# Two adaLN pairs of the second layer computed during the routing of the first layer's experts

## The reference, cut to what matters

```python
def trunk(x, cond, P, caches):
    for l in range(2):
        mod = silu(cond) @ P['ada_w'][l] + P['ada_b'][l]          # (1024) @ (1024, 6144)
        sh1, sc1, g1, sh2, sc2, g2 = split(mod, 6)
        h = x * (1.0 + sc1) + sh1
        out = even_mixer(h, ...) if l % 2 == 0 else hyena_mixer(h, ...)   # hyena: u = h @ hy_w_in ...
        x = layer_norm(ALPHA * x + g1 * out, ln_w[l, 0], ln_b[l, 0])
        h = x * (1.0 + sc2) + sh2
        y = moe_ffn(h, router_w, router_bias, moe_w_gate[l], moe_w_up[l], moe_w_down[l])
        x = layer_norm(ALPHA * x + g2 * y, ln_w[l, 1], ln_b[l, 1])
```

## Time and profile before

| | us |
|---|---|
| median of 3 runs | 1306.19 |
| lowest, highest | 1302.87, 1306.76 |
| the profiled execution | 1303.92 |
| its span, first to last instruction | 1302.2 |
| TensorE busy | 991.1 (76%) |
| VectorE busy | 415.4 (32%) |
| ScalarE busy | 228.1 (18%) |
| GpSimd busy | 164.3 (13%) |
| read from memory | 320.50 MB |

### The profile page before, as it was taken

The page is one execution under the profiler, slowest core; times in us unless marked ns, Lnnn a source line. Parts: engine busy times, 40 slices in busy tenths (PEclk is TensorE's granted clock), DMA queues, the critical chain, the costliest instruction groups (busy, mean ns, idle before and its releaser), DMA issues.

```text
span 1302.2 us, 23736 instructions
## 1 busy us (share of the span) xinstructions
PE 991.1 (76%) x9370; PEld 553.3 (42%) x9370; DVE 415.4 (32%) x1135; ACT 228.1 (18%) x455; POOL 164.3 (13%) x323
## 2 busy tenths in 40 slices
PE   1899998698289759794489999898938997775830
PEld 0444446554245435352245554445424553332510
DVE  0220117855422212121453234553541221111207
ACT  0401002513212111121221111110321211110202
POOL 1200001100221111112020000001022111110121
PEclk9999999799689989898799998899958998887965
DMA  9995324577379999999994113633631969999973
GB/s 323 374 306 204 105 108 137 195 310 290 152 281 388 395 396 394 404 367 390 392 377 150 45 60 104 257 130 138 254 158 41 329 245 393 401 407 404 391 275 133
DMA packets 78858, 345.06 MB, mean 265 GB/s; under 512 B 8086, under 2 KB 8537, under 8 KB 66508
## 3 DMA queue, kind: packets, MB, share of 16 engines
q1 hardware_dynamic: 57108, 289.30, 57.6%
q0 software_dynamic: 13648, 43.84, 9.9%
q10 hardware_dynamic: 8040, 11.01, 2.5%
HBM read 320.50 MB, written 23.63 MB: 264 GB/s over the span
## 4 chain that ended last, share of the span: by engine, by line
PE 57%; DMA 23%; DVE 11%; ACT 3%; issue 2%; SPq 2%; POOL 1%; POOLq 0%; ACTq 0%; DVEq 0%; PEldq 0%
DMA ring<-in_moe_w_up_dram 15%; PE bank L830 15%; PE bank L636 11%; PE bank L895 10%; PE bank L759 6%; PE bank L837 6%; DMA ring<-in_ada_w_dram 5%; PE bank L589 2%; SPq L1323 2%; DMA ring<-in_moe_w_down_dram 1%; PE bank L969 1%; PE bank L993 1%; ACT arena L1181 1%; PE bank L907 1%; DVE arena L1292 1%
## 5 line engine op out<-in xcount | busy, mean ns | idle before, releaser
L830 PE MATMUL bank<-ring,arena 128*32 128x256 f32 x3072 | 193.9, 409 | 51.7 <-DMA ring<-in_moe_w_up_dram 49.5
L830 PEld LDWEIGHTS bank<-ring,arena 128*32 128x32 f32 x3072 | 105.0, 118 | 133.4 <-issue 76.1
L636 PE MATMUL bank<-ring,hT 128*128 128x512 f32 x336 | 144.9, 593 | 1.0 <-ACT hT L1029 1.0
L1290 DVE TENSOR_TENSOR arena<-arena,bank 128x64 f32<-128x64 f32 x136 | 27.4, 201 | 316.1 <-ACT arena L1181 316.1
L895 PE MATMUL bank<-hT,ring 128*128 128x384 f32 x384 | 124.6, 487 | 1.0 <-ACT hT L1029 1.0
L837 PE MATMUL bank<-ring,arena 128*32 128x256 f32 x1536 | 92.8, 382 | 27.5 <-DVE arena L1292 25.4
L589 PE MATMUL bank<-ring,small 128*32 128x256 f32 x768 | 55.5, 453 | 62.1 <-DMA ring<-in_ada_w_dram 62.1
L636 PEld LDWEIGHTS bank<-ring,hT 128*128 128x128 f32 x336 | 63.6, 190 | 80.6 <-issue 79.3
L895 PEld LDWEIGHTS bank<-hT,ring 128*128 128x128 f32 x384 | 72.7, 190 | 52.5 <-ACT hT L1029 1.2
L830 PE MATMUL bank<-arena 128*32 128x256 f32 x1216 | 74.3, 399 | 14.8 <-DMA arena<-in_moe_w_up_dram 14.8
L837 PEld LDWEIGHTS bank<-ring,arena 128*32 128x32 f32 x1536 | 45.1, 109 | 58.6 <-DVE arena L1292 31.9
(11 more groups left out here) (316 smaller groups left out, 1093.9 us busy)
## 6 DMA issues: line engine op xcount, KB each, us to landing
ring<-in_ada_w_dram SPq DMA_DIRECT2D x24, 2048.0 KB, 19.1
ring<-in_moe_w_gate_dram SPq DMA_DIRECT2D x22, 2048.0 KB, 22.0
ring<-in_moe_w_up_dram SPq DMA_DIRECT2D x22, 2048.0 KB, 27.0
ring<-in_moe_w_down_dram SPq DMA_DIRECT2D x22, 2048.0 KB, 29.9
arena<-in_moe_w_gate_dram SPq DMA_DIRECT2D x10, 2048.0 KB, 35.6
arena<-in_moe_w_up_dram SPq DMA_DIRECT2D x10, 2048.0 KB, 41.3
arena<-in_moe_w_down_dram SPq DMA_DIRECT2D x10, 2048.0 KB, 44.3
ring<-in_ev_w_in_dram SPq DMA_DIRECT2D x7, 2048.0 KB, 16.4
```

The costliest lines, as they stand in the source:

```text
L636: last = pe.matmul(bank[3 * (c % 2) + t], hT[:, k, t * P:(t + 1) * P], slot8(n)[:, k, :], start=k == 0, stop=k == KT - 1)
L830: last = pe.matmul(bank[1][q * BLK:(q + 1) * BLK, 0:HALF], slot_inT[:, k, :], both[:, :, k, q * P:(q + 1) * P], start=k == 0, stop=k == KT ...
L1290: dve.tensor_tensor(act_rows[:, two, :], silu_g[:, two, :], up, ALU.mult).then_inc(S["gated"], 1)
```

## The change

The four chunks of pairs (1,0) and (1,1) move from the head of `BETWEEN` to the end of `BEFORE`. They are loaded to slots 4, 6, 7 and 8: the three last ones where expert 2 was loaded before, the first to slot 4 once the mixer's output is through with it. Both pairs are computed within `pe_moe` of layer 0, behind the position counts and the token copies, in banks 3, 4 and 2. Their rows can't lie in slot 5, which an expert takes, so they are written to the head of `hT`, whose content the token copies have used up. Expert 0, expert 1's gate and expert 1's down are loaded as before the routing; expert 1's up and expert 2's three matrices wait for the ada matmuls. In `BETWEEN` the slots of the later chunks shift, so that the chunks of (1,2) and (1,3) now have slots 3, 4, 0, 1 and come first. In the gap only (1,2) and (1,3) are left; the copies of (1,0) and (1,1) are gone from `act_ln`, (1,2) is copied before the wait for tile 0's scale, and the columns of (1,3) are made behind the modulate.

```diff
--- before.py
+++ after.py
@@ -65,8 +65,9 @@
 
 
 BEFORE = (pair_chunks(0, 0) + pair_chunks(0, 1) + matrix_chunks("ev_in", 0, 3) + pair_chunks(0, 3) + matrix_chunks("ev_in", 3, 7)
-          + pair_chunks(0, 2) + pair_chunks(0, 4) + pair_chunks(0, 5) + matrix_chunks("ev_out", 0, 2))
-BETWEEN = (pair_chunks(1, 0) + pair_chunks(1, 1) + pair_chunks(1, 2) + pair_chunks(1, 3) + matrix_chunks("hy_in", 0, 6)
+          + pair_chunks(0, 2) + pair_chunks(0, 4) + pair_chunks(0, 5) + matrix_chunks("ev_out", 0, 2)
+          + pair_chunks(1, 0) + pair_chunks(1, 1))
+BETWEEN = (pair_chunks(1, 2) + pair_chunks(1, 3) + matrix_chunks("hy_in", 0, 6)
            + pair_chunks(1, 4) + pair_chunks(1, 5) + matrix_chunks("hy_out", 0, 2))
 MOE0 = len(BEFORE)
 HYBRID1 = MOE0 + 3 * NE
@@ -76,8 +77,8 @@
 
 def ring_slots():
 
-    slots = [(i + 4) % STAGING for i in range(len(BEFORE))] + [i % MOE_RING for i in range(3 * NE)]
-    slots += [(i + 3) % STAGING for i in range(len(BETWEEN) - 5)] + [0, 1, 2, 3, 4] + [i % MOE_RING for i in range(3 * NE)]
+    slots = [(i + 4) % STAGING for i in range(len(BEFORE) - 4)] + [4, 6, 7, 8] + [i % MOE_RING for i in range(3 * NE)]
+    slots += [(i + 3) % STAGING for i in range(len(BETWEEN) - 6)] + [3, 4, 0, 1, 3, 4] + [i % MOE_RING for i in range(3 * NE)]
     seen = [0] * MOE_RING
     held, full, before = [None] * MOE_RING, [], []
     for n, slot in enumerate(slots):
@@ -569,10 +570,13 @@
         def dve_proj_count(c):
             return sum(2 if k in ROPED else 0 for k in range(c + 1))
 
+        def mod_row_of(l, q):
+            return at(q * HALF, HALF, src=hf) if l == 1 and q < 2 else mod_rows[q]
+
         def act_ada(act, l, q, b):
 
             act.wait_ge(ada_mm, ADA_ORDER.index((l, q)) + 1)
-            act.activation(mod_rows[q], b[:, 0:HALF], ACT.Copy).then_inc(mod_row, 1)
+            act.activation(mod_row_of(l, q), b[:, 0:HALF], ACT.Copy).then_inc(mod_row, 1)
 
         def pe_condition(pe):
             pe.wait_ge(cond_act, 1)
@@ -598,7 +602,7 @@
 
             pe.wait_ge(mod_row, ADA_ORDER.index((l, q)) + 1)
             for j in range(2):
-                last = pe.transpose(b[:, j * P:(j + 1) * P], mod_rows[q][:, j * P:(j + 1) * P], ident)
+                last = pe.transpose(b[:, j * P:(j + 1) * P], mod_row_of(l, q)[:, j * P:(j + 1) * P], ident)
             last.then_inc(modT_mm, 1)
 
         def dve_ada_columns(dve, l, q, b):
@@ -813,6 +817,11 @@
                 last = pe.matmul(bank[6][:, NT * NE:(NT + 1) * NE], ones, mask[:, s, :], start=s == 0, stop=s == NT - 1)
             last.then_inc(pos_mm, 1)
             pe.wait_ge(htok_act, 6 * (l + 1))
+            if l == 0:
+                pe_ada(pe, 1, 0, bank[3])
+                pe_ada(pe, 1, 1, bank[4])
+                pe_ada_columns(pe, 1, 0, bank[2])
+                pe_ada_columns(pe, 1, 1, bank[3])
             pe.wait_ge(table_rdy, l + 1)
             pe.wait_ge(trips_rdy, l + 1)
 
@@ -887,6 +896,7 @@
                     pe.wait_ge(hy_dve, c - 2)
                 if c == 2:
                     pe.wait_ge(dft_in, 16 * 4)
+                    pe.wait_ge(modT_rdy, COLUMN_PAIRS.index((1, 3)) + 1)
                     pe.matmul(bank[7][0:FH, 0:T], w1, feat, start=True, stop=True).then_inc(fmm, 1)
                 if c == 5:
                     pe.wait_ge(fsin, 1)
@@ -1040,21 +1050,17 @@
 
         def act_ln(act, n):
             j = n // 2
-            if n == 1:
-                act_ada(act, 1, 0, bank[0])
             for t in range(NT):
-                if n == 1 and t == 2:
-                    act_ada(act, 1, 1, bank[1])
                 act.wait_ge(gathered[t], 32 * (j + 1))
                 act.activation(ln_sum(n, t), ln_sum(n, t), ACT.Copy, scale=wsel[:, 0, t:t + 1]).then_inc(ln_first, 1)
             for t in range(NT):
                 act.wait_ge(ln_var, NT * j + t + 1)
                 act.activation(sd[:, t:t + 1], mv[:, t, 1:2], ACT.Sqrt, bias=eps_col, scale=1.0).then_inc(ln_sd, 1)
                 if t == 0:
+                    if n == 1:
+                        act_ada(act, 1, 2, bank[2])
                     act.wait_ge(ln_rstd, j + 1)
                     act.activation(ln_sum(n, 0), ln_sum(n, 0), ACT.Identity, bias=nmr[:, 0:1], scale=rstd[:, 0:1]).then_inc(ln_nrm, 1)
-                    if n == 1:
-                        act_ada(act, 1, 2, bank[2])
             if n == 1:
                 act_ada(act, 1, 3, bank[7])
 
@@ -1170,6 +1176,9 @@
                 act.wait_ge(htok_mm, 6 * l + u + 1)
                 act.activation(h_tok[:, u // 2, :].rearrange("p (k j s) -> p j s k", k=KT, j=KT)[:, u % 2 * 4:u % 2 * 4 + 4],
                                bank[u].rearrange("p (j s k) -> p j s k", j=4, k=KT), ACT.Copy).then_inc(htok_act, 1)
+            if l == 0:
+                act_ada(act, 1, 0, bank[3])
+                act_ada(act, 1, 1, bank[4])
             act.wait_ge(trips_rdy, l + 1)
             act.sem_inc(S["stored0"], 32)
             act.sem_inc(S["stored1"], 32)
@@ -1278,6 +1287,9 @@
             link(dve.tensor_reduce(places[:, FIRST:NE], square, AX, ALU.add))
             link(dve.tensor_scalar(places[:, FIRST:NE], places[:, FIRST:NE], -1.0, float(NE), ALU.mult, ALU.add))
             dve.tensor_copy(order[0:1, FIRST:NE], places[0:1, FIRST:NE]).then_inc(order_rdy, 1)
+            if l == 0:
+                dve_ada_columns(dve, 1, 0, bank[2])
+                dve_ada_columns(dve, 1, 1, bank[3])
             dve.wait_ge(trips_rdy, l + 1)
             pairs = dve.value_load(trips[0:1, 1:2], min_val=NE // 2, max_val=MAX_BLOCKS // 2)
 
@@ -1330,21 +1342,42 @@
                 else:
                     sp.wait_ge(MS[layer]["down_mm"], ends)
 
+            def staging_free(layer):
+                sp.wait_ge(modT_mm, 4 * (layer + 1))
+                sp.wait_ge(gate_out[2 * layer], 64)
+                sp.wait_ge(gate_out[2 * layer + 1], 64)
+
+            def first_experts():
+
+                gap = chunk_at("ada", 1, 0)
+                for j in range(3):
+                    sp.wait_ge(*used(PREVIOUS[MOE0 + j]))
+                    expert_matrix(sp, 0, 0, MOE0, j)
+                sp.wait_ge(cT_mm, KT)
+                sp.wait_ge(out_done, 16 * OUT_DMAS)
+                for n in range(gap + 1, gap + 4):
+                    sp.dma_start(slot8(n), chunk_src(n)).then_inc(ring_full[SLOT[n]], 16)
+                sp.wait_ge(*used(PREVIOUS[MOE0 + 3]))
+                expert_matrix(sp, 0, 1, MOE0 + 3, 0)
+                load(gap)
+                staging_free(0)
+                expert_matrix(sp, 0, 1, MOE0 + 3, 2)
+                for e, j in ((1, 1), (2, 0), (2, 1), (2, 2)):
+                    sp.wait_ge(*used(PREVIOUS[MOE0 + 3 * e + j]))
+                    expert_matrix(sp, 0, e, MOE0 + 3 * e, j)
+
             def load_moe(layer, first):
 
-                for e in (0, 2, 1):
-                    if e == 2 and layer == 0:
-                        sp.wait_ge(cT_mm, KT)
-                        sp.wait_ge(out_done, 16 * OUT_DMAS)
-                    if e == 2 and layer == 1:
+                if layer == 0:
+                    first_experts()
+                for e in (0, 2, 1) if layer else ():
+                    if e == 2:
                         sp.wait_ge(inv_dve, KT)
                         sp.wait_ge(lnrow_in, ROWS_DUE[2])
                     for j in range(3):
                         n = first + 3 * e + j
                         if SLOT[n] == STAGING:
-                            sp.wait_ge(modT_mm, 4 * (layer + 1))
-                            sp.wait_ge(gate_out[2 * layer], 64)
-                            sp.wait_ge(gate_out[2 * layer + 1], 64)
+                            staging_free(layer)
                         elif SLOT[n] < STAGING:
                             sp.wait_ge(*used(PREVIOUS[n]))
                         expert_matrix(sp, layer, e, first + 3 * e, j)
@@ -1363,7 +1396,7 @@
                         next_expert(three * 3 + group, group)
                 next_expert(NE - 1, 0)
 
-            for n in range(MOE0):
+            for n in range(MOE0 - 4):
                 load(n)
             load_moe(0, MOE0)
             for n in range(HYBRID1, MOE1):
@@ -1444,14 +1477,10 @@
             pe_projections(pe)
             pe_mixer(pe)
             pe_moe(pe, 0, MOE0)
-            pe_ada(pe, 1, 0, bank[0])
-            pe_ada(pe, 1, 1, bank[1])
-            pe_ada_columns(pe, 1, 0, bank[0])
             pe_ada(pe, 1, 2, bank[2])
-            pe_ada_columns(pe, 1, 1, bank[1])
             pe_ada(pe, 1, 3, bank[7])
+            pe_modulate(pe, 2)
             pe_ada_columns(pe, 1, 3, bank[7])
-            pe_modulate(pe, 2)
             pe_hyena(pe)
             pe_moe(pe, 1, MOE1)
 
@@ -1733,9 +1762,8 @@
             dve_tiles(dve, link, 0)
             dve_moe(dve, link, 0)
             dve_ln(dve, link, 1)
-            for q, b in ((0, 0), (1, 1), (3, 7)):
-                dve_ada_columns(dve, 1, q, bank[b])
             dve_modulate(dve, 2)
```

(1 more changed line is left out.)

## The result

The changed kernel takes 1311.26 us (median of 20 runs), the kernel before 1306.32 us (20 runs): ratio 1.0043, 95% interval 1.0027 to 1.0059, so 3.5 to 7.7 us slower. The forecast was 1310.5, +4.5. The profiled execution of after was timed at 1313.39 us, its span is 1311.7. In its trace everything stands 1.8 us later already where the first scatter is issued (345.08 instead of 343.32). Executions differ by as much there without any change: in experiment 7, whose edit lies wholly behind this place, the scatter is issued at 345.92. So I compare places by their distance from that issue.

A forecast was written before the change was run, and what follows sets the result against it. Bound by waits for ada weights between the first expert layer and the projection, a 65.9 us gap. Scatters' delay +19.5 minus gap gain 15.0 is +4.5 on 1306.2: 1310.7, rounded to 1310.5 us, range 1298.5 to 1316.5.

The forecast's parts named there:

- The loads beside the scatters: In the routing, four late expert matrices take turns by packet with the scatters, which end 19.5 us later.
- The share by bytes: Rival, 20 in 100: scatters get half the bytes in the routing, start +11.0 us, net -4.0, 1302.2 us.
- the scatters' right of way: Rival, 11 in 100: scatters hardly slowed in the routing, expert layer on time, four matrices late; middle -11.5, 1294.7 us.
- the fetch's 4.6 us: First row fetch after the scatters: 7.0 us beside a full queue instead of 2.4, looking more like one fixed delay.
- It reaches the end: First expert layer: the 19.5 us later start carries through in full to the last down product.
- everything is shifted: First expert layer: everything to the last down product moves by 19.5 us and nothing in it is shortened.
- the 18 to 21 of the range: Bounds, in us, on how much later the scatters in the routing end.
- what the prediction only touched in a rival: First expert layer starts on time, but the four matrices are late, so expert 3's loads begin 0 to 7 us later.
- Computation in the routing: Routing: the two moved pairs' matmuls, copies and column operations are hidden by 8 us of TensorE idling; cost 0.
- The gap: Between first expert layer and hyena projection: fewer chunks and copies, gain 15.0 us, bounds 13.5 and 16.5.
- the modulate behind TensorE's idling: In the gap: restarting after idling costs the modulate 1 us, bounds 0 and 2.4, beyond its usual 4.24.
- the chunks that leave the queue: In the gap: four 2 MB chunks no longer queue, so pairs (1,2) and (1,3) land when the old ones did.

The follow-up runs named there:

- experiment 7: Kernel before, with the copies of pairs (1,0) and (1,1) put behind the scaling of the three tiles, loads and matmuls unmoved: 1307.63 us, ratio 1.0018.
- experiments 2 and 3: Changed kernel with each of the four late matrices loaded by four DMAs (4 KB packets): 1305.54 us; by eight (2 KB packets): 1299.14 us.
- Experiment 4: Kernel before, with only expert 1's up and expert 2's three matrices issued as late as the scatters, no pair moved: 1319.62 us, ratio 1.0118.
- Experiment 6: Changed kernel with the four late matrices held until the scatters have landed and the first two blocks of rows are fetched: 1307.09 us, ratio 1.0006.
- experiment 1: Changed kernel, but SyncE issues the four late expert matrices only after the six scatters have landed: 1303.54 us, ratio 0.9979.
- experiment 5: Changed kernel without the four chunks' loads, both pairs computed from expert 0's matrices, experts loaded as before: 1287.38 us, ratio 0.9847.

## Why the prediction was right

*The loads beside the scatters, forecast +19.5, measured +20.85.* The step held as it was put: the share of the queues goes by packets. The estimate had the turns start at 345, with 25.5 us of turns and 3.2 us for the rest. In the trace even turns start only at 350, since GpSimd's queue comes in late, and the last two matrices are issued 8.9 us behind the first scatter, not 6.5. Neither matters much beside 16 KB packets: there are 864 scatter packets and 576 of the matrices (small ones included; the prediction had counted 768 and 512), so the scatters' are the last in either case, and they end when all 11.5 MB are through. That is also why the bounds were narrow. What decided it between the rivals is the packet size, and experiments 2 and 3 show it directly: 32.5, 23.1, 17.9 us. The share by bytes is out (23.1 us would have been there from the start), and so is the scatters' right of way. The remark that the fetch's 4.6 us look like one fixed delay was right in part. The fetch waits 7.34 us beside 16 KB packets, 4.72 and 4.74 beside 4 and 2 KB packets, and 1.79 alone: some 3 us hardly depend on the packets' size, the rest does.

*It reaches the end, forecast in full, measured +21.3 at the last down product.* Experiment 4 has it apart from the rest: +17.8 at the first block, +20.9 at the last down product. So the delay isn't lost on the way, but "everything is shifted" is too neat: there it grew by 3 us. +21.3 is also just above the 18 to 21 of the range. Experiment 6 adds what the prediction only touched in a rival: with an early first block the four matrices themselves are late, and experiment 1, which merely protects the scatters, keeps 10.8 us of the 21.3.

*Computation in the routing, forecast 0, measured 0.* First block 17.31 against 17.29 in experiment 5. The second pair was cheaper than reckoned wherever the matrices were held: its 64 matmuls took 3.63 us in experiment 1, not 5.99.

*The gap, forecast -15.0, measured -14.1.* The second tile's scaling, from the end of the last down product: 24.5 us before, forecast and measured. The last `x` tile 45.7 us behind it, forecast 45.6. The term that was too small is the modulate behind TensorE's idling: 678.21 - 672.25 = 5.96 us against 4.24, so 1.7 where I took 1, inside the bounds. The granted clock in the stretch 671 to 675 us was 0.50, which is the lower of its two levels (1.2 of 2.4 GHz), and TensorE had done almost nothing from 667 to 671. Its 22 transposes took 4.96 us there; in the kernel before, where the stretch 665 to 669 was granted 1.00, 24 took 3.23:

```profile
667.00:671.00 4.00, 0.33 (x1) 0.14 (x1) 3.86 (x8) 0.56 (x2) 0.00 (x0) 0.98 1.05 386
671.00:675.00 4.00, 2.75 (x13) 2.75 (x14) 2.37 (x4) 1.83 (x4) 2.50 (x5) 0.50 1.05 388
```

(The columns are the stretch, its length, busy us and instructions of PE, PEld, DVE, ACT and POOL, granted clock, DMA share, GB/s.) What I said of the source of the gain, the chunks that leave the queue, is borne out by experiment 7.

*The sum.* +4.5 forecast, +4.9 by the medians, +3.5 to +7.7 by the ratio. The mechanism and both terms held, but that the total agrees to half a us is luck. In the traces the delay came out 1.8 us larger and the gain 0.9 us smaller than named, both to the same side, and the terms add up to +7.2.

## What to carry to other kernels

Half-empty queues are not free for a large load if small packets on the critical path pass at the same time: count the packets of both queues. Here each got one in turn (123 and 123 in 5 us), so each 4 KB packet waited for 16 KB of the other queue. Put the large load ahead of the critical transfer or behind it, or cut it into small pieces: held behind it gave 1303.5 us, in 2 KB packets 1299.1, half ahead and half behind 1293.4 to 1295.5, against 1311.3 beside it. And a load that is moved forward pushes others back: here four weights that nobody missed before the experts began were the ones that made the experts late.

## What the runs showed of the hardware

A queue that becomes active beside a full one came in late, on top of the turns: 3 of 85 packets from 345 to 350 us in the changed kernel (16 KB), 9 of 313 from 346 to 350 with 4 KB packets. With empty queues the first scatter packet starts 1.7 us behind the first issue (before and experiment 1). It started 4.8 us behind it beside 16 KB packets (the changed kernel and experiment 4), 5.3 beside 4 KB and 3.3 beside 2 KB. So the late start itself is worth 1.5 to 3.6 us, and not the same for each size; its cause is open.

In the changed kernel TensorE's second pair also ended late. From the timeline of after, and of experiment 1, where the matrices were held:

```profile
344.72 5.06 PE L593 MATMUL bank<-arena,small 128*32 128x256 f32 x64
...
353.99 0.38 ACT L579 ACTIVATE hT<-bank 128x256 f32<-128x256 f32 x1 [8.64 <-remote]
```

```profile
344.69 3.63 PE L593 MATMUL bank<-arena,small 128*32 128x256 f32 x64
...
348.83 0.38 ACT L579 ACTIVATE hT<-bank 128x256 f32<-128x256 f32 x1 [3.50 <-PE bank L597]
```

The copy comes 5.2 us later, though no weight was missing. With 2 KB and 4 KB packets the 64 matmuls took 3.64 us, so something that TensorE needed seems to come late beside 16 KB packets alone. The queues' record has one candidate: q8, of kind "instruction", moves a single packet of 16 KB in this stretch, at 349.7 us in the changed kernel and at 346.3 in experiment 1, so 5.0 and 1.6 us behind the pair's start. But with 4 KB packets it comes 4.1 us behind it and nothing is slowed. That it is the cause isn't shown, and no run was spent on it. The delay cost nothing here, since it lay inside the hole that the scatters left.
